# Clearing the expert rows' scratch from the mixer stage, and a last inverse level that is multiplied from two half-width buffers

## The reference, cut to what matters

```
lmat = where(strict, einsum('nbhid,nbhjd->nbhij', kb, k) * decay, 0)
tinv = triangular_solve(eye + lmat, eye)       # u = tinv @ vb, w = tinv @ (kb * exp(gc))
v_new = u_i - w_i @ S
o_i   = qg_i @ S + a_i @ v_new
...
for e in range(N_EXP):                          # top-2 gates, zero for the others
    out = out + gates[..., e:e+1] * _swiglu(h, w_gate[e], w_up[e], w_down[e])
```

## Time and profile before

| | us |
|---|---|
| median of 3 runs | 1474.06 (1471.61 to 1477.42) |
| profiled execution, its own time | 1471.61 |
| its span, first to last instruction | 1469.9 |
| mixer stage from first level to V_new | about 190 to 246 |
| dense SwiGLU | about 299 to 530 |
| expert layer, loads of 2 MB | about 600 to 1450 |

### The profile page before, as it was taken

The page is one execution under the profiler, slowest core; times in us unless marked ns, Lnnn a source line. Parts: engine busy times, 40 slices in busy tenths (PEclk is TensorE's granted clock), DMA queues, the critical chain, the costliest instruction groups (busy, mean ns, idle before and its releaser), DMA issues.

```text
span 1469.9 us, 28089 instructions
## 1 busy us (share of the span) xinstructions
PE 1370.1 (93%) x12664; PEld 719.5 (49%) x12664; DVE 324.3 (22%) x402; ACT 303.2 (21%) x400; POOL 87.5 (6%) x168
## 2 busy tenths in 40 slices
PE   5999889879999998999989999999999999999974
PEld 1995587568888876343323333333343343343322
DVE  1444654654544445000000000000000000000005
ACT  2435453443343433000000010100001001000001
POOL 5100132420000001000000000000000000000010
PEclk9899999989999998999999999999999999999998
DMA  8846717989565549999999999999999999999994
GB/s 337 284 173 273 284 60 287 358 323 355 182 198 173 198 139 419 394 423 424 421 424 424 399 383 349 363 419 423 407 420 424 401 421 424 398 423 423 421 421 165
DMA packets 125474, 501.29 MB, mean 341 GB/s; under 512 B 10748, under 2 KB 14664, under 8 KB 103856
## 3 DMA queue, kind: packets, MB, share of 16 engines
q1 hardware_dynamic: 110464, 471.98, 81.1%
q10 hardware_dynamic: 12208, 18.12, 3.4%
q0 software_dynamic: 2688, 9.47, 1.6%
HBM read 479.86 MB, written 19.69 MB: 340 GB/s over the span
## 4 chain that ended last, share of the span: by engine, by line
PE 72%; DMA 8%; SPq 3%; DVE 2%; ACT 1%; issue 1%; ACTq 0%; DVEq 0%
PE ps L2056 31%; PE ps L2104 12%; PE ps L382 6%; PE ps L383 6%; PE ps L384 6%; PE ps L2099 3%; PE ps L1587 3%; SPq L505 3%; DMA ring_b<-in_moe_down 2%; DMA ring_a<-in_moe_down 2%; DMA ring_b<-in_moe_gate 2%; DMA raw<-in_moe_down 2%; PE ps L1601 1%; PE ps L1812 1%; PE ps L1803 1%
## 5 line engine op out<-in xcount | busy, mean ns | idle before, releaser
L2056 PE MATMUL ps<-ring_a,hTf 128*32 128x512 f32 (+1 forms) x2192 | 216.1, 544 | 5.1 <-DMA ring_a<-in_moe_up 3.9
L1546 DVE TENSOR_TENSOR hm<-gate_bc,ps 128x512 f32<-128x512 f32 (+1 forms) x44 | 27.3, 622 | 824.1 <-PE ps L2056 823.0
L2056 PE MATMUL ps<-raw,hTf 128*32 128x384 f32 (+1 forms) x2032 | 198.0, 540 | 3.7 <-DMA raw<-in_moe_up 3.2
L354 DVE TENSOR_TENSOR w_lo<-raw,w_hi 128x2048 fp32r<-128x2048 f32 x60 | 137.6, 2306 | 155.7 <-ACT w_hi L350 155.7
L2056 PE MATMUL ps<-ring_b,hTf 128*32 128x512 f32 (+1 forms) x1408 | 140.9, 545 | 5.3 <-DMA ring_b<-in_moe_gate 3.0
L350 ACT ACTIVATE w_hi<-raw 128x2048 fp32r<-128x2048 f32 x60 | 113.7, 1912 | 114.6 <-PE ps L384 112.7
L2056 PEld LDWEIGHTS ps<-ring_a,hTf 128*32 128x32 f32 x2192 | 68.4, 110 | 136.5 <-issue 124.5
L2056 PEld LDWEIGHTS ps<-raw,hTf 128*32 128x32 f32 x2032 | 64.5, 110 | 121.8 <-issue 115.2
L382 PE MATMUL ps<-w_hi,hTh 128*128 128x512 f32 x288 | 114.5, 397 | 9.7 <-DVE w_lo L354 4.6
L383 PE MATMUL ps<-w_hi,hTl 128*128 128x512 f32 x288 | 113.6, 395 | 0.0
L384 PE MATMUL ps<-w_lo,hTh 128*128 128x512 f32 x288 | 113.5, 394 | 0.0
(11 more groups left out here) (353 smaller groups left out, 1474.8 us busy)
## 6 DMA issues: line engine op xcount, KB each, us to landing
raw<-in_w_mod SPq DMA_DIRECT2D x48, 1024.0 KB, 6.9
raw<-in_moe_down SPq DMA_DIRECT2D x23, 2048.0 KB, 23.9
ring_a<-in_moe_down SPq DMA_DIRECT2D x19, 2048.0 KB, 23.4
ring_a<-in_moe_gate SPq DMA_DIRECT2D x14, 2048.0 KB, 21.7
ring_b<-in_moe_down SPq DMA_DIRECT2D x14, 2048.0 KB, 24.2
raw<-in_moe_up SPq DMA_DIRECT2D x12, 2048.0 KB, 23.9
ring_a<-in_moe_up SPq DMA_DIRECT2D x12, 2048.0 KB, 24.5
raw<-in_moe_gate SPq DMA_DIRECT2D x10, 2048.0 KB, 16.4
```

Source lines behind the costliest of these rows:

```text
L354: nc.vector.tensor_tensor(w_lo[:, w % SPLIT], raw[:, slot % RAW], w_hi[:, w % SPLIT].bitcast(F32), ALU.subtract).then_inc(s["lo_ready"], 1)
L2056: last = MM(ps[TOK * j:TOK * j + TOK, part % 4, 0:w], hTf1[:, kt, q * P + TOK * g:q * P + TOK * g + TOK], wt[:, kt % 2, j, :], start=kt == ...
```

## The change

- The last level no longer goes to `LT`. The near diagonal block stays in `XTd`, the far one and the negated off-diagonal block go to `XL`, the unused second half of `XT`. V_new becomes 32 matmuls: for each block one 64*64 (`XTd[near, i]`) and one over 128 rows and 64 columns (`XL[:, i]`).
- GpSimd's two memsets of `LT`, their waits and TensorE's wait for them go; `mask_attn` follows the last level mask directly.
- `zeros` is now `b_ch[:, 10:12]`, memset by GpSimd when the values have been transposed out of it (`v_turned`), ahead of the level masks.
- ScalarE issues the clearing transfer right after it has saved the first matrices of the inversion, ahead of all `save_xt` and `save_m1`. The wait for `rows_cleared` moves to GpSimd ahead of `fetch_gate(1)` and to ScalarE ahead of the copies of the turned `y`; the later waits of GpSimd and VectorE go.

```diff
-        zeros = hm[:, 0]
+        zeros = b_ch[:, 10:12].rearrange("p a n -> p (a n)")
...
+            pool.wait_ge(s["v_turned"], 1)
+            nc.gpsimd.memset(zeros, 0.0).then_inc(s["attn_masked"], 1)
...
-            pool.wait_ge(s["m1_turned"], 16)
-            for d in range(2):
-                cut = LT.rearrange("p (b d h) n -> p b d h n", b=NB, d=2)[strips[1 - d], :, d, :, strips[d]]
-                pool.wait_ge(s["ct_ready"], 2 * LAST + d)
-                nc.gpsimd.memset(cut, 0.0).then_inc(s["ct_ready"], 1)
-            pool.wait_ge(s["ct_ready"], 2 * LAST + 2)
             for b in range(NB):
                 mask_attn(b)
...
+            pool.wait_ge(s["rows_cleared"], 16)
             fetch_gate(1)
...
-            step(nc.gpsimd.memset(zeros, 0.0))
...
                 last.then_inc(s["LT_saved"], 1)
+            act.wait_ge(s["attn_masked"], 2)
+            act.dma_start(rows_io.rearrange("(p k) (h n) -> p (k h) n", p=P, n=512), rep(zeros, 1, 2 * REGION * N_EXP // P))\
+                .then_inc(s["rows_cleared"], 16)
...
-                    for part in (near, far):
-                        last = nc.scalar.activation(LT[part, 4 * g:4 * g + 4, part],
-                                                    ps[part, 2 + g % 2, 0:256].rearrange("p (i n) -> p i n", n=HB), ACT.Copy)
+                    nc.scalar.activation(flat2(XTd[near, 4 * g:4 * g + 4]), ps[near, 2 + g % 2, 0:256], ACT.Copy)
+                    last = nc.scalar.activation(flat2(XL[far, 4 * g:4 * g + 4]), ps[far, 2 + g % 2, 0:256], ACT.Copy)
...
-                        last = MM(block(4, g, i, near), M1d[far, i], LT[far, i, far], start=True, stop=True)
+                        last = MM(block(4, g, i, near), M1d[far, i], XL[far, i], start=True, stop=True)
...
-            pe.wait_ge(s["ct_ready"], 2 * LAST + 2)
...
-                    last = MM(ps[:, g % 2, (i % 4) * P:(i % 4 + 1) * P], LT[:, i], R[:, i], start=True, stop=True)
+                    cut = slice((i % 4) * P, (i % 4 + 1) * P)
+                    MM(ps[near, g % 2, cut], XTd[near, i], R[near, i], start=True, stop=True)
+                    last = MM(ps[far, g % 2, cut], XL[:, i], R[:, i], start=True, stop=True)
```

More of the change, by code:

```diff
@@ L252, in build @@
         CT = (blocks(X, 8), blocks(LT, 8))
+        XL = blocks(XT, 8)
         LO = flat2(M1[:, 4:8]).rearrange("p (i n) -> p i n", n=HB)
@@ L724, in _ @@
             pool.wait_ge(s["route_ready"], 1)
-            pool.wait_ge(s["rows_cleared"], 16)
             for b in range(NB):
@@ L978, in _ @@
             copy_rows(4, 3)
+            act.wait_ge(s["rows_cleared"], 16)
             act.wait_ge(s["y_turned"], 2)
@@ L995, in _ @@
             fetch(w_rt[:, :, 0:N_EXP], w_router[0].rearrange("(t p) e -> p t e", p=P), "poolw_loaded")
-            act.dma_start(rows_io.rearrange("(p k) (h n) -> p (k h) n", p=P, n=512), rep(zeros, 1, 2 * REGION * N_EXP // P))\
-                .then_inc(s["rows_cleared"], 16)
             def ffn_silu(i_gate):
@@ L1322, in update_level @@
                         part = strips[g % 2]
-                        nc.vector.tensor_scalar(LT[part, cut, strips[1 - g % 2]], out[part], -1.0, None, ALU.mult).then_inc(s["xx_saved"], 1)
+                        nc.vector.tensor_scalar(XL[part, cut], out[part], -1.0, None, ALU.mult).then_inc(s["xx_saved"], 1)
             update_level(0)
@@ L1549, in _ @@
             passes = nc.vector.value_load(npass[0:1, 0:1], min_val=1, max_val=3)
-            dve.wait_ge(s["rows_cleared"], 16)
             with dve.Fori(0, passes) as p:
@@ L1815, in turn_attn @@
             def turn_attn(b):
-                pe.wait_ge(s["attn_masked"], 2 + b)
+                pe.wait_ge(s["attn_masked"], 3 + b)
                 pe.wait_ge(s["attnT_saved" if b else "mod_cols_saved"], 1 if b else 4)
@@ L1863, in _ @@
                     pe.wait_ge(s["vnew_saved"], g - 1)
+                near, far = strips[g % 2], strips[1 - g % 2]
                 for i in range(4 * g, 4 * g + 4):
-                    last = MM(ps[:, g % 2, (i % 4) * P:(i % 4 + 1) * P], LT[:, i], R[:, i], start=True, stop=True)
+                    cut = slice((i % 4) * P, (i % 4 + 1) * P)
+                    MM(ps[near, g % 2, cut], XTd[near, i], R[near, i], start=True, stop=True)
+                    last = MM(ps[far, g % 2, cut], XL[:, i], R[:, i], start=True, stop=True)
                 last.then_inc(s["vnew_turned"], 1)
```

## The result

The changed kernel took 1493.06 us (median of 4 runs, 1490.95 to 1497.62) against 1473.02 us for the kernel before on the same chip (4 runs): a ratio of 1.0135, with a 95% interval of 1.0102 to 1.0168. It is 20 us slower, and outside the range of 1471 to 1489. The profiled execution of after was near the slow end, 1497.07 us with a span of 1495.3; 8.1 us of its distance to the profiled run of before lie ahead of the first edit, where the granted clock was lower (0.87 in place of 0.93 over 16 to 190). I therefore compare stretches, not the two spans.

What follows compares the result with a forecast made beforehand. TensorE was taken to bound the kernel (72% of the span). Terms -1.6 + 0.6 + 4 + 2 + 1 = +6.0 on 1471.61 gave 1477.6, as a median 1480 us, with a range of 1471 to 1489.

Steps and rivals of the forecast that it cites:

- part 5: V_new in 32 matmuls: tile halves mostly overlap, so +1 us, lower end 0.
- part 3: Inversion: TensorE's instruction packets meet DMA engines filled by the clearing and stall it, +4 us, bounds 0 and +8.
- The product drains: Rival on V_new: every change between 64*64 and 128*64 empties the array, +8 in place of +1, 1487; chance 0.28.
- Part 1: Inversion: GpSimd's memsets go and `mask_attn` moves up, ending TensorE's idle wait for VectorE before level 4's transposes, -1.6 us.
- Part 2: Start of the inversion: ScalarE's early issue of the clearing delays the first L924, +0.6 us, between 0 and 0.9.
- Part 4: L1601 after level 4: modulation unit loads land late beside the clearing, +2 us, bounds 0 and 5.7.
- The clearing is cheap where it is put: Rival: packets and loads get through in time, parts 3 to 5 cost nothing, 1473; chance 0.20.
- The SwiGLU gains: Rival: clearing caused the SwiGLU's lower clock and late `w_lo`, so some 9 us come back, 1464; chance 0.09.

Runs made afterwards that it cites:

- product_paired: Changed kernel with the clearing at its old place and V_new's groups taken two at once, equal tile shapes side by side: 1473.41 us, ratio 0.9997.
- clear_only: Kernel before with only the clearing transfer, its zeros and its waits moved as in the change: 1489.91 us, ratio 1.0105.
- experiment 5: Kernel before with half of the `rows_io` clearing issued early, half at the old place; its trace also examined for the clock: 1484.65 us, ratio 1.0075.
- clear_half: Kernel before with one half of `rows_io` cleared early and the other half at the old place: 1484.65 us, ratio 1.0075.
- product_only: Changed kernel with the clearing back at its old place: 1479.46 us, ratio 1.0030.
- mask_early: Kernel before with only GpSimd's two `mask_attn` calls moved ahead of its memsets of `LT`: 1474.32 us, ratio 0.9999.
- product_grouped: Changed kernel with the clearing at its old place and each V_new group's four near tiles multiplied before its four far ones: 1477.89 us, ratio 1.0026.
- clear_in_swiglu: Kernel before with the clearing issued one turn of ScalarE's SwiGLU loop later: 1477.11 us, ratio 1.0017.

## Why the prediction was wrong

The sum was +6.0 and the change costs +20.0. One step had the wrong mechanism, part 5, and one term was far too small, part 3.

**Part 5, V_new: the step that failed.** I took +1, an overlap of the two halves, "near the overlap rows, since they speak of the same sharing". They didn't: L1601's column groups have one shape, and the product alternates two. The measured term is +7.6, the price of "The product drains" (+8), and its arithmetic held too, 0.14 for a change where the earlier trace rows gave 0.26 there and back. `product_paired` shows the overlap where the shapes are equal. The Trainium skill's rule ("TensorEngine Tiling (Array Packing)", Key Properties), that a change of tiling mode drains TensorE, agrees with these traces at 0.14 us a change. So of this step the rival was right, and it had 0.28.

**Part 3, instruction packets: mechanism right, term mis-sized.** I had +4 within 0 and +8. Measured: 11.6 us of stops in place of 2.5, which is +9.1, and about +4.5 for the groups behind them at 1.2 GHz (6.2 and about 6 in `clear_only`). The size went wrong twice. I took the mean of "0 and 2.0" as a packet's price from two that met single loads, while beside a DMA that stays full the stops took 1.7 to 3.75 us in after and 1.0 to 3.4 in `clear_only`. And I counted nothing for a lower clock, part of which may be chance (experiment 5). I had also passed over a small stop of before, 0.45 us at 195.95. That packets are what TensorE waits for is an inference, since the profile has no releaser for "issue", but a strong one. The early clearing alone brings the stops, and the stop of before goes when a load is held. Counted through the trace of after, weight loads and waits included, the four begin behind TensorE's records 2497, 2753, 3009 and 3521, which are 256, 256 and 512 apart; those of `clear_only` and `clear_half` begin behind the same four numbers, and the two of before behind the first and the last of them. And each of the four in after ends 1.4 to 1.5 us behind the end of a packet of the instruction queue: the packets end at 206.39, 213.42, 220.96 and 234.08, TensorE goes on at 207.75, 214.85, 222.43 and 235.56. The fifth packet, which ends at 227.85, stops nothing; TensorE had just been in the longer matmuls of L1847. The Trainium skill ("Runtime: NRT & Kernel Launch", Instruction fetch mechanics) has blocks of 256 instructions, which agrees, and a crossing that is "mostly hidden", which does not agree with four of the five here: 1.7 to 3.75 us each.

**Part 1, the masks: right in mechanism, the size not told from the straying of the levels.** -1.6 was forecast; `product_only` and `mask_early` have levels 1.7 and 2.1 us shorter than before, `product_grouped` and `product_paired`, with the same order, 0.9 and 0.4 longer. VectorE's first two products went from 2.9 and 2.8 to 1.22 and 0.69, and no wait for VectorE stands between the levels in after. The Trainium skill ("SBUF — State Buffer", Who interferes with whom) calls the port pair that VectorE and GpSimd share an exclusive lock, and this agrees: with two inputs from SBUF on both sides both were slow (VectorE's 2.91 in place of 1.22, the two masks 5.66 in place of 4.67), and with one input from PSUM (L1333 in after) VectorE took 0.68 beside a mask as without.

**Part 2, the issue: 0 in place of +0.6.** I had it start when L905 ends (L902 in after) and delay the first L924. In the list it does stand there, but ScalarE's queue issued it at 197.25, while the engine was still in the copies L896 and ahead of the first L902, and the issue took 0.64 us, not 1.74. The copies follow without a gap:

```profile
197.25 0.64 ACTq L907 DMA_DIRECT2D rows_io<-b_ch  x1
197.85 1.56 ACT L902 ACTIVATE T<-ps 64x256 f32<-64x256 f32 x4
200.34 0.85 ACT L923 ACTIVATE T<-ps 128x256 f32<-128x256 f32 x2 [0.92 <-PE ps L1810]
```

The wait ahead of L923 is 0.92, as it was 0.93.

**Part 4, the modulation units: 0 in place of +2.** TensorE came to them 12 us later than before, when the clearing had landed (236.9). L1599 takes 3.57 at 252.68, with no wait for a transfer. I had named this way out, "if part 3 is true TensorE comes later", and yet kept the 2.

By the terms of the traces, with about -2 for the masks: -2 + 0 + 9.1 + 4.5 + 0 + 7.6 = +19.2, against 20.0 between the medians. With the levels straying by 2 us the closeness is in part luck. "The clearing is cheap where it is put" falls with `clear_only` (+14.6). "The SwiGLU gains" falls with after, where TensorE's weights stand the same 4.88 us, and with `clear_in_swiglu`. The low chance of 0.41 for slower came from the middle of a sum whose two largest terms had upper ends of +8 each. One came out at 7.6 and the other beyond its end, at 13.6, and together they passed the range.

## What to carry to other kernels

A stretch in which the DMA engines are idle isn't free room for a long transfer if TensorE runs short matmuls there. By all that these runs show it went through its instructions so fast that it had to wait for the next packet of them, and those came late beside the transfer. The same 12 MB beside matmuls of 512 columns left TensorE busy for 57.00 of 57.00 us. Before a move of a transfer, follow who overwrites its source and what else is issued on its queue, since those wait for its landing, and its landing depends on what it shares the engines with (39.6, 52.7 and 64.4 us here). Cutting a product into smaller tiles was no gain here while their shapes alternated (11.2 us against 3.6); with equal shapes side by side it came near the old time (5.1), not below.

## What the runs showed of the hardware

- Issuing a transfer on a queue whose 12 MB transfer is still running held the issuing engine for 34.13 us; moved to another queue the same store held ScalarE for none (one run each).
- A change between 64*64 and 128*64 tiles cost 0.14 us, and each record of a half-width tile 0.109, nearly that of one of full width (3.72 us for 32 records, 0.116 each). Tiles of one shape on different parts of the array ran side by side, 16 records in 1.02 us.
- Beside the full DMA engines TensorE stopped for 1.0 to 3.75 us behind records that are 256 or 512 apart, and in after went on 1.4 to 1.5 us behind the end of an instruction packet.
- Behind the four stops of 3.39 us or more TensorE ran some microseconds at 1.2 GHz; behind shorter ones, 1.85 to 2.65 us, it did so in some traces and not in others.
